# Attention of four layers issued between weight blocks, masks and biases added in VectorE's maximum pass, top-k steps spread, output blocks begun in part

## The reference

```python
for blk in range(seq // Q_BLOCK):                       # layer 1: MLA, 8 heads | stick-breaking, 8 heads
    p_a = softmax(where(chunk_ok, q_a @ k_a * scale_a, -inf));  o_a = p_a @ v_a
    z = q_b @ k_b * scale_b
    log_keep = where(before, log_sigmoid(-z), 0);  log_between = cumsum_reversed(log_keep) - log_keep
    w_b = where(before, exp(log_sigmoid(z) + log_between), 0);   o_b = w_b @ v_b
h = h + concat(o_a, o_b) @ w_out;   h = h + swiglu(rms_norm(h))
# layer 2: 16 heads, scores + rel_bias[clip(q - k)], a chunk of 64 sees itself and what lies before; swiglu
# layer 3: 16 query heads on 4 key heads; an indexer of 8 heads scores all keys and the best 64 are kept:
score = einsum('qh,qhs->qs', w_blk, relu(qi @ ki));  idx = top_k(where(causal, score, -inf), 64)
p = softmax(where(valid, q @ k[idx] * scale, -inf));  h = h + (p @ v[idx]) @ w_out;  h = h + relu(h @ w1)**2 @ w2
# layer 4: 16 heads over 272 keys, with a forgetting decay c = cumsum(log_sigmoid(f)):
p = softmax(where(causal, q @ k * scale + c[q] - c[k], -inf));  h = h + (p @ v) @ w_out;  then relu(..)**2 MLP
```

## Time and profile before

| | |
|---|---|
| median of three runs | 1466.47 us (1453.88 to 1475.46) |
| profiled execution, first to last instruction | 1499.4 us |
| PE busy | 1444.6 us (96%), weight loads 1319.4 |
| DVE busy | 824.1 us (55%) |
| ACT busy | 740.2 us (49%) |
| POOL busy | 357.1 us (24%) |
| moved by DMA | 213.77 MB, mean 143 GB/s |
| mean granted TensorE clock | 0.918 of full |

### The profile page before, as it was taken

One profiled execution on the slowest core, in us unless ns is written; L12 is line 12 of the kernel. 1 busy time (PEld: TensorE's weight loads), 2 busy tenths in 40 slices (PEclk: granted clock), 3 DMA queues, 4 the chain that ended last, 5 costly groups with the idle time before them and its releaser, 6 DMA issues.

```text
span 1499.4 us, 29006 instructions
## 1 busy us (share of the span) xinstructions
PE 1444.6 (96%) x10577; PEld 1319.4 (88%) x10577; DVE 824.1 (55%) x1348; ACT 740.2 (49%) x1357; POOL 357.1 (24%) x380
## 2 busy tenths in 40 slices
PE   6978999999989999999989999999999999999999
PEld 5965999999976899999867579999999855799999
DVE  5576655565543655557488346555556532455544
ACT  5355666655323566665244345444346633454433
POOL 1011244411000144422313005770000000177400
PEclk9997999999986999999998569999999955799999
DMA  7521465565541355566323015555554400255665
GB/s 235 161 92 43 133 190 187 183 214 183 175 160 29 105 169 188 182 204 205 105 84 113 1 45 166 169 174 187 172 168 147 147 1 1 85 170 186 195 188 159
DMA packets 61652, 213.77 MB, mean 143 GB/s; under 512 B 7840, under 2 KB 9888, under 8 KB 61440
## 3 DMA queue, kind: packets, MB, share of 16 engines
q1 hardware_dynamic: 60304, 210.10, 44.4%
q10 hardware_dynamic: 1264, 2.49, 0.6%
HBM read 211.51 MB, written 1.05 MB: 142 GB/s over the span
## 4 chain that ended last, share of the span: by engine, by line
PE 90%; issue 3%; DVE 3%; ACT 2%; DMA 1%; POOL 1%; SPq 0%; POOLq 0%; DVEq 0%; ACTq 0%
PE bank L320 24%; PE bank L318 24%; PE bank L319 24%; PE bank L853 3%; PE bank L852 2%; PE bank L882 2%; PE bank L881 1%; PE bank L868 1%; PE bank L883 1%; PE bank L870 1%; PE bank L869 1%; PE bank L976 1%; DVE wlo L304 0%; PE bank L1421 0%; DMA raw<-stream 0%
## 5 line engine op out<-in xcount | busy, mean ns | idle before, releaser
L304 DVE TENSOR_TENSOR wlo<-raw,whi 128x1024 fp32r<-128x1024 f32 x394 | 484.2, 1229 | 147.0 <-ACT whi L299 146.3
L318 PE MATMUL bank<-uhi,whi 128*128 128x256 f32 (+1 forms) x1848 | 532.0, 288 | 17.1 <-DVE wlo L304 14.1
L299 ACT ACTIVATE whi<-raw 128x1024 fp32r<-128x1024 f32 x394 | 414.2, 1052 | 252.1 <-PE bank L320 249.5
L320 PE MATMUL bank<-uhi,wlo 128*128 128x256 f32 (+1 forms) x1848 | 526.3, 285 | 0.0
L319 PE MATMUL bank<-ulo,whi 128*128 128x256 f32 (+1 forms) x1848 | 525.7, 284 | 0.0
L318 PEld LDWEIGHTS bank<-uhi,whi 128*128 128x128 f32 x1848 | 351.3, 190 | 19.2 <-issue 14.2
L320 PEld LDWEIGHTS bank<-uhi,wlo 128*128 128x128 f32 x1848 | 351.3, 190 | 0.0
L319 PEld LDWEIGHTS bank<-ulo,whi 128*128 128x128 f32 x1848 | 349.6, 189 | 1.1
L318 PE MATMUL bank<-ahi,whi 128*128 128x256 f32 (+1 forms) x1224 | 349.8, 286 | 0.0
L319 PE MATMUL bank<-alo,whi 128*128 128x256 f32 (+1 forms) x1224 | 347.7, 284 | 0.0
L320 PE MATMUL bank<-ahi,wlo 128*128 128x256 f32 (+1 forms) x1224 | 347.5, 284 | 0.0
(11 more groups left out here) (230 smaller groups left out, 1482.1 us busy)
## 6 DMA issues: line engine op xcount, KB each, us to landing
raw<-stream SPq DMA_DIRECT2D x394, 512.0 KB, 3.6
scratch<-relh ACTq DMA_DIRECT2D x8, 256.0 KB, 2.6
constants<-consts SPq DMA_DIRECT2D x1, 1264.0 KB, 11.6
h<-xT SPq DMA_DIRECT2D x4, 256.0 KB, 4.3
out<-h SPq DMA_DIRECT2D x8, 128.0 KB, 2.8
scratch<-sel ACTq DMA_DIRECT2D x1, 384.0 KB, 3.5
h<-metaT SPq DMA_DIRECT2D x1, 64.0 KB, 10.7
gain_columns<-gains SPq DMA_DIRECT2D x1, 45.0 KB, 1.9
```

The costliest lines, as they stand in the source:

```text
L299: act.activation(whi[:, s, :], raw[:, s, :], ACT.Copy).then_inc(w_hi, 1)
L304: dve.tensor_tensor(wlo[:, s, :], raw[:, s, :], whi[:, s, :].bitcast(F32), ALU.subtract).then_inc(w_lo, 1)
L318: pe.matmul(dst, hi, a, start=first and i == 0, stop=False)
L320: mm = pe.matmul(dst, lo, a, start=False, stop=last and i == chunks - 1)
```

## The change

The order of the units is changed so that attention can go on between them, and so is the order of all four engines' queues.

- Layer 1: phases `sq`, `sk`, `mla` become one, `mix`, with the order q0 k0 m0 m1 q1 k1 m2 m3 ... m6 m7 (`MIX`). Stick-breaking and MLA attention of pair s stand between the units of s and s+1 (`mix_pe`). For the m units ACT and DVE split only 640 of the 1024 columns (`mix_ahead`). The two diagonal masks of a head are multiplied in one instruction.
- Layer 2: `bq` and `bk` become `bqk`, alternating. `band_pe` issues, per pair, q unit, turning of pair s-2, scores of pair s-1, k unit, values of pair s-2.
- Layer 4: `fk` and `fq` become `fkq`, alternating; `fox_pe` does the same with the statistics between; the split of the second normalisation (`second_u_*`) moves into `fv`. The 16 meta keys' values are matmuls of 128 rows, the rest of them cleared to zero by POOL.
- Layer 3: `dsa_*` replaces `proj_*` there: the indexer's pairs stand behind units 6 to 9, DVE's part of them one unit later, two top-k steps in each of the units 10 to 19. Its attention still stands behind all units.
- Heads go in pairs: scores of both heads are issued alternately (`pair_scores_pe`), values too (`pair_values_pe`).
- No mask or bias is a matmul any more. `biased_max_dve` adds a tile from SBUF in the maximum pass and writes the negated sums to `prob`, from where ACT takes the exponential. The tiles: a constant (MLA), the score tiles (indexed), `relh` with the mask in it, 384 instead of 256 columns a head (band), and the decay: written to DRAM once, broadcast back to 128 partitions for each pair by ACT's queue, the causal part added by POOL (`decay_pool`).
- Output units 0 to 3 are begun before the last pairs are done (`part`, `out_part_pe`) on banks of their own (`OUT_BANKS`).
- Start: unit 0 is loaded ahead of the last two pieces of x; ACT does all eight multiplied columns first, then the squares; the norm's matmul stands behind unit 2; two `sv` units fill the wait for the latent norms.

```diff
-    ("cq", 3), ("ckv", 2), ("kr", 1), ("sv", 4), ("sq", 4), ("sk", 4), ("mla", 8), ("out0", 8),
+    ("cq", 3), ("ckv", 2), ("kr", 1), ("sv", 4), ("mix", 16), ("out0", 8),
...
+        def pair_scores_pe(pe, a, s):
+            pair = (2 * s, 2 * s + 1)
+            if a.head0 + 2 * s > 0:
+                pe.wait_ge(s_max, 2 * (a.head0 + 2 * s))
+            for i in pair:
+                pe.matmul(bank[4 + i % 2][:, 0:a.w0], a.q(i)[:, 0:128], a.k(i)[:, 0:a.w0], start=True, stop=True,
+                          skip_group_check=True)
+            for i in pair:
+                pe.matmul(bank[4 + i % 2][:, a.w0:a.w0 + a.w1], a.q(i)[:, 128:256], a.k(i)[:, 0:a.w1], start=True, stop=True,
+                          skip_group_check=True).then_inc(s_ready, 1)
...
+        def biased_max_dve(dve, a, i):
...
+            for t, (c0, w) in enumerate(((0, a.w0), (a.w0, a.w1))):
+                more = score[t][:, 0:w] if a is dsa else add[:, c0:c0 + w]
+                dve.tensor_tensor_reduce(out=a.p[:, i % 2, c0:c0 + w], in0=sc[:, c0:c0 + w], in1=more,
+                                         scale=-1.0, scalar=-NEG, op0=ALU.add, op1=ALU.min,
+                                         accum_out=a.nmx[:, i % 2, t:t + 1]).then_inc(s_max, 1)
...
+        def band_pe(pe):
+            a, n0, b0, last = band, START["bqk"], BSTART["bqk"], band.pairs - 1
...
+            for s in range(a.pairs):
+                unit(2 * s)
+                if s >= 2:
+                    pair_turn_pe(pe, a, s - 2)
+                if s >= 1:
+                    scores(s - 1)
+                unit(2 * s + 1)
+                if s >= 2:
+                    pair_values_pe(pe, a, s - 2)
+            pair_turn_pe(pe, a, last - 1)
+            scores(last)
+            out_part_pe(pe, "out1", a, 0, 0, 6, FIRST)
+            pair_values_pe(pe, a, last - 1)
+            out_part_pe(pe, "out1", a, 1, 0, 6, FIRST)
+            pair_turn_pe(pe, a, last)
...
+            for s in range(a.pairs):
+                unit(2 * s, inside=(lambda s=s: stat(2 * s - 1)) if s else None)
+                if s >= 2:
+                    pair_turn_pe(pe, a, s - 2)
+                if s >= 1:
+                    scores(s - 1)
+                if s:
+                    stat(2 * s)
+                unit(2 * s + 1, inside=None if s else lambda: stat(0))
+                if s >= 2:
+                    pair_values_pe(pe, a, s - 2)
...
+                for n in range(2 * TOPK_STEPS * (i - 10) // 10, 2 * TOPK_STEPS * (i - 9) // 10):
+                    if n >= 0:
+                        topk_step(dve, link, n // TOPK_STEPS, n % TOPK_STEPS)
```

More of the change, by code:

```diff
@@ L312, in unit_mm @@
             for i in range(chunks):
+                if inside is not None and i == 5:
+                    inside()
                 if x is not None:
@@ L320, in unit_mm, with chunks_mm @@
                 mm = pe.matmul(dst, lo, a, start=False, stop=last and i == chunks - 1)
+            if used:
+                mm.then_inc(w_used, 1)
+        def chunks_mm(pe, n, dst, xhi, xlo, cols, chunks, ready, first, last, used):
+            s = n % RING
+            pe.wait_ge(w_lo, n + 1)
+            for i in chunks:
+                pe.wait_ge(*ready(i))
+                hi, lo = (w[:, s, i * P:(i + 1) * P] for w in (whi, wlo))
+                a, b = xhi[:, i, cols], xlo[:, i, cols]
+                pe.matmul(dst, hi, a, start=first and i == chunks[0], stop=False)
+                pe.matmul(dst, hi, b, start=False, stop=False)
+                mm = pe.matmul(dst, lo, a, start=False, stop=last and i == chunks[-1])
             if used:
@@ L454, in resid_pe, with resid_act @@
                 group(it)
[L456 removed]
+        def resid_act(act, link, name, kc, cols, norm, gname, ahead=0):
             per = -(-kc // DC)
@@ new lines, in decay_act, with decay_pool @@
+        def decay_act(act, s):
+            act.dma_start(cb[:, s % 2, :, :], decay[2 * s:2 * s + 2, :].partition_broadcast(P)).then_inc(c_loaded[s % 2], 16)
+        def decay_pool(pool, s):
+            diag = cb[:, s % 2, :, :].rearrange("p b n -> p (b n)")
+            pool.wait_ge(c_loaded[s % 2], 16 * (s // 2 + 1))
+            for i in range(2):
+                for c in (416 * i + META, 416 * i + META + T):
+                    pool.tensor_tensor(diag[:, c:c + P], diag[:, c:c + P], const("causal"), ALU.add).then_inc(c_masked, 1)
@@ new lines, in stick_z_pe @@
+        def stick_z_pe(pe, s):
+            pe.wait_ge(evac, MIX_EVAC["k", s])
+            if s > 0:
+                pe.wait_ge(z_arg, 2 * s)
+                pe.wait_ge(z_olo, s)
+            q, k = ([half(x[:, s, FIRST], b) for b in range(2)] for x in (sbq, sbk))
+            for b in range(2):
+                pe.matmul(bank[2 + b][:, 0:256], k[b][:, 0:128], q[b], start=True, stop=True)
+            for b in range(2):
+                mm = pe.matmul(bank[2 + b][:, 256:384], k[b][:, 128:256], q[b][:, 128:256], start=True, stop=True)
+            mm.then_inc(z_ready, 1)
@@ new lines, in stick_arg_dve, with stick_weights_dve @@
+        def stick_arg_dve(dve, s):
+            dve.wait_ge(z_sum, s + 1)
+            for b in range(2):
+                dve.tensor_tensor(ls[:, b, :], ls[:, b, :], bank[2 + b][:, 0:384], ALU.add).then_inc(z_arg, 1)
+        def stick_weights_dve(dve, s):
+            for b in range(2):
+                dve.wait_ge(z_exp, 2 * s + b + 1)
+                x = diagonals(zlog[:, b, :])
+                dve.tensor_tensor(x, x, const("before").rearrange("p (c n) -> p c n", n=P), ALU.mult).then_inc(z_w, 1)
@@ L1695, in _ @@
+            for s in (0, 1):
+                decay_act(act, s)
+            fox_act(act, link)
+            resid_act(act, link, "out3", DC, FIRST, 7, "mlp1", ahead=1)
             sqrelu_act(act, "up3", FIRST)
```

1653 lines of the change are left out of this document (1004 added, 649 removed), and 4 rows, old and new, of the table PHASES.

## The result

The changed kernel takes 1340.64 us (median of four, 1339.63 to 1344.44) against 1470.97 for the kernel before (1453.88 to 1498.34): ratio 0.917, interval 0.909 to 0.926. The ratio and its interval leave out the slow executions of the kernel before (over 1.5% above its fastest); the two medians as they stand would give 0.911. The forecast was 1304 in a range of 1268 to 1362: right in direction and inside the range, 37 us too low.

The account below looks back on a forecast made before the run. The four attention stages were taken as bound by TensorE, mostly at half clock, the indexed projections by DVE. Terms -43 -65 -24 -31 -5 made -168 of 1499.4 us; the same share of the 1466.5 median gave 1302, stated as 1304, range 1268 to 1362.

Parts of the forecast that it names:

- Band, -43: Band layer: from 112.7 us, a woven step of 8.4 us eight times plus 2 us of ends, clock staying at 2.4 GHz.
- The dear end for the scores (apart, +7): Band: if a pair's scores don't run side by side, they cost 1.70 us instead of 0.85, 7 us more.
- Forgetting layer, -65: Forgetting layer: from 155.3 us to about 90, eight steps of 10.4 us plus 6 us of waits.
- the 6 us of waits: Forgetting layer: 6 us added because ACT and DVE work in strict order, with two normalisations and a softmax in one chain.
- First layer and start, -24 and -5: First layer from 101.7 to 78 us; at the start, first matmul 4 us earlier and a 1.46 us wait filled.
- the 7 us added for gaps: First layer: 7 us added to PE's 71 us for gaps in a chain through three engines.
- Indexed layer, -14 and -17: Indexed layer: DVE-bound projections lose half their 29 idle us, -14; attention at clock 0.50 falls to 51 us, -17.
- rival (b): Indexed attention: the clock recovers there as well, -16 us, giving 1288 us; chance 0.10.
- rival (a): Woven stages: DVE becomes the bound, by a dear maximum or its strict order; price 35 us, giving 1340; chance 0.25.
- The biased maximum, +0.15: DVE: the maximum becomes an operation and an accumulator read, 112 times, each 0.15 us dearer; bounds 0 and 0.62.
- Begun output blocks, 14 us of cover: Layer ends: begun blocks cover the last pair's chain; if they cover nothing, each layer waits 3 to 4 us, 14 us.
- The same share of the median: Last step: the 11.2% gain on the profiled span applied to the 1466.5 us median, 164 us off, giving 1302.

Follow-up runs that it names:

- The flat runs: Changed kernel with the band's 16 q and k blocks first, its eight pairs behind them: 1362.3 us; the same with twelve useless matmuls ahead of each turning: 1359.7 us.
- one mended order: Changed kernel with DVE's split of a pair's result ahead of the next maxima in the indexed attention, nothing else: 1333.9 us.
- The second profile: The kernel before, unchanged, measured and profiled again: 1478.5 us, the profiled execution with a span of 1474.0.

## Why the prediction was right or wrong

**What bounds the kernel: the rows right, the reading half right.** PE was busy from end to end at half clock, and the sum priced that well. But from busy at half clock the text took that the clock was the loss. The flat runs show a second bound behind it: in the changed kernel's band at full clock a pair costs 2.4 us of PE and 4.8 of its chain. While PE was busy at half clock that chain didn't show; weaving covers it and keeps the clock at 1.00.

**Band, -43: measured -42.3.** The step came out at 8.35 us for 8.4. Its parts are a little off both ways: turning 0.75 for 0.96, the two blocks 5.94 for 5.8. The dear end for the scores (apart, +7) is closed. A change of tile does cost something. In the step shown above the distances between starts are:

```profile
398.63 0.29 PE L332 MATMUL bank<-uhi,wlo 128*128 128x256 f32 x1
398.75 0.27 PE L873 MATMUL bank<-constants,prob 128*128 128x128 f32 x1
...
399.30 0.27 PE L875 MATMUL bank<-constants,prob 128*128 128x128 f32 x1
399.50 0.49 PE L946 MATMUL bank<-scratch 64*128 64x128 f32 x4
...
400.35 0.39 PE L330 MATMUL bank<-uhi,whi 128*128 128x256 f32 x1
400.58 0.28 PE L331 MATMUL bank<-ulo,whi 128*128 128x256 f32 x1
```

From a block to the turning, both 128*128, it is 0.12 us as within the block. From the turning to the scores, 128*128 to 64*128, it is 0.20 us for 0.11, and in the block behind the scores the second matmul starts 0.23 us after the first, elsewhere 0.12. Each of the four changes in a step shows two such places of 0.05 to 0.11 us more, some 0.7 us of the 8.35. Much of it was in the start-to-start times of the earlier trace rows already, which hold such changes too; what came on top is the 0.14 us by which two blocks exceed twice 2.9, 1 us in the band, not 11 over all stages. That the two row halves run side by side, which the forecast took from the earlier trace rows, held: 0.86 us for the scores of two heads, in either order of issue. The trace shows delays at the changes of tile, some 0.2 us a change, and not what they come from.

**Forgetting layer, -65: measured -61.6.** The step of 10.6 us is as summed, and the 6 us of waits were 5.6: 0.97, 0.78 and 0.81 in the first pairs, 2.04 and 1.01 at the last statistic. What is left over lies in the ends.

**First layer and start, -24 and -5: measured -30.3 together.** The first matmul came 2.1 us earlier (11.93, not 14.05), forecast 4, and the last plain block of the start ended 1.8 earlier. That the first block "ran at half clock" isn't what the trace says: its 5.26 us are that pace, a matmul every 0.213 us, but the granted clock from 14.05 to 19.31 was 1.00, and so it was in the changed kernel from 11.93 to 17.30, at the same pace. The layer made up for what the start didn't give: PE was busy 78.3 of 80.3 us, so most of the 7 us added for gaps wasn't needed. The MLA scores of a pair, 96 rows a head, took 1.41 us (85.81 to 87.22) for the same 384 columns a head that cost 0.86 with 64 rows; 1.7 were forecast.

**Indexed layer, -14 and -17: measured -30.5.** The projections gave 8.7 us (102.9 to 94.2), not 14; DVE stayed the bound with 76.3 us. The attention with its output blocks gave 21.8, not 17: the clock came back in its second half (0.82 on the mean), which is rival (b) in part. Some of what the clock gave a new wait took: DVE's split stood behind the maxima, and PE waited 6.8 us for it. That order, splits behind a maximum, is in rival (a); that the maxima would wait for the turning, because they now write `prob`, is named nowhere in the prediction.

**The biased maximum, +0.15: measured +0.08** (0.083 for the read, the operation 0.36 as the plain one). Rival (a), whose 1340 us is the time that came, has DVE as the bound of the woven stages. That didn't happen: 40 us more on DVE cost the band and the first layer under 1 us, the forgetting layer 5 to 7. Only its strict order showed, and that in the indexed attention, which isn't woven (7 to 12 us won back by one mended order). The number agrees by chance.

**Begun output blocks, 14 us of cover: less.** Of "each of the four layers has 3 to 4 us of wait at its end" the band has 3.3 (2.8 in the layer's time) and the forgetting layer 2.0, of which nothing shows in its time; the other two weren't tried.

**The step that failed is the last: "The same share of the median".** The sum gives 1499.4 - 168 = 1331 us for the changed span, measured 1337.8: 0.5% off. Scaling by 1466.5 / 1499.4 took off another 29 us. That would be right if a profiled execution were longer everywhere. The second profile shows where it is longer: in the attention at low clock, which is what the change removes, while the MLP stretches, which stay, repeat to 0.02 us. The excess must be subtracted from the gain, not shared out over what is left: the gain in runs is 1471 - 1341 = 130 us, in the profiled executions 162. Done so, the forecast would have been 168 - 33 = 135 us below 1466.5, which is 1331 again, 9 us under the measured time; the range held the time because it was wide. The rest of the error, 6 us, is the forgetting layer's 3.4 and the MLP stretches' 3.1 (two of them 1.5 us longer, each with a clock of 0.96 in the first 45 us; why it is lower there wasn't found).

## What to carry to other kernels

Forecast the time after from what stays, plus the new work, and not as the median less a share: a profiled execution may be off its median, and the excess sits in some stretches only; find these with a second profile. When PE is busy at half clock, work out the chain of the other engines too: here it was the next bound, 4.8 us a pair for 2.4 of PE's. Weaving independent weight blocks between its links covered it (22.3 us in the band), where the mask matmuls taken away in place gave at most 27 of some 143 us. When an operation begins to write a buffer that it only read before, look at who still reads it: here that made a wait in the one stage that had no cover.

## What the runs showed of the hardware

TensorE, busy from end to end by modelled ends, stayed at a granted clock of 0.50 for 95.7 us of small matmuls in the forgetting attention, and at 0.56 for 80.0 us without the masks. In the changed kernel's flat band the clock went from 0.61 to 1.00 when twelve wide matmuls a pair were added. Weight matmuls of 256 columns started every 0.213 us at 0.50 (changed kernel, 455.1 to 458.3) and every 0.120 us at 1.00. The first is 1.2 columns a ns, so the 1.2 GHz of the forecast is an estimate, at one column a cycle, and its 2.4 is twice that; the pace at 1.00 is 2.1 columns a ns. The first block of each of these two kernels had the slower pace, 0.213 us, at a granted clock of 1.00.

The same program, the kernel before, had mean clocks of 0.915 to 0.957 and times that fell with them, 1506.2 to 1447.7 us; its two profiles differ in the attention stages (9.7, 9.6 and 4.3 us), while the MLP stretches repeat within 0.02 us. DVE's read of its accumulator takes 0.083 us here, ACT's 0.187 (0.196 in the kernel before). Two heads' half-height scores overlap even when issued one head after the other (0.86 us for both, 64 rows a head; 1.41 with 96 rows). At a change between 128*128, 64*128 and 128*64 tiles two starts come 0.05 to 0.11 us late each; at one between a rounded and a plain fp32 matmul of the same tile the next start came after 0.12 us, as within the block.
